# First mixing stage of a two-block kernel: decay and keys early, the triangular inverse in pieces, attention and linear-attention units in one loop

## The reference

```
p = h @ ab_w_in                              # q, k, v of the attention | r, k, v, w, a, g of the other
# differential attention, per head, causal, in blocks of 128 queries
s = q_c . k_c (c = 0, 1);  p_c = softmax(mask(s_c))
attn = p_0 - lam_full * p_1;  o = rmsnorm(attn @ v) * (1 - lam_init)
# the other one (RWKV-7 time mix): token shift with mu, then per step
decay = exp(-exp(-0.5) * sigmoid(w0 + tanh(p_w) @ w2)); a = sigmoid(a0 + p_a @ a2)
kk = normalise(k * k_k); k = k * (1 + (a - 1) * k_a)
S = S * decay - (S kk) (kk * a)^T + v k^T;   y = S r
out = (groupnorm(y) + sum(r * k * r_k) * v) * g
```

## Time and profile before

| | us |
|---|---|
| median of 3 runs | 2768.85 (2764.5 to 2778.71) |
| profiled execution, its own time | 2759.99 |
| its span in the profile | 2758.2 |
| TensorE busy in the span | 2653.2 (96%) |
| VectorE, ScalarE, GpSimd busy | 1453.7, 985.1, 528.3 |
| mean granted clock of TensorE | 0.977 |

### The profile page before, as it was taken

One profiled execution on the slowest core, in us unless ns is written; L12 is line 12 of the kernel. 1 busy time (PEld: TensorE's weight loads), 2 busy tenths in 40 slices (PEclk: granted clock), 3 DMA queues, 4 the chain that ended last, 5 costly groups with the idle time before them and its releaser, 6 DMA issues.

```text
span 2758.2 us, 32180 instructions
## 1 busy us (share of the span) xinstructions
PE 2653.2 (96%) x13236; PEld 2112.1 (77%) x13236; DVE 1453.7 (53%) x1905; ACT 985.1 (36%) x1660; POOL 528.3 (19%) x554
## 2 busy tenths in 40 slices
PE   8989998999999998899999999999999998999998
PEld 7777877788888665686788888888878745888886
DVE  8875995643434688546433334343354466533432
ACT  3235545422323533543322223222233445322221
POOL 5711001322200020101222102221002124222200
PEclk9999999999999998899999999999999989999999
DMA  4433112222232231002232332323323300222332
GB/s 154 100 96 113 62 46 69 84 100 93 96 102 93 71 99 32 28 2 69 100 100 92 95 104 92 99 98 93 102 78 122 116 16 1 78 98 99 97 93 86
DMA packets 76932, 232.19 MB, mean 84 GB/s; under 512 B 14961, under 2 KB 16241, under 8 KB 76529
## 3 DMA queue, kind: packets, MB, share of 16 engines
q1 hardware_dynamic: 64176, 212.46, 23.8%
q0 software_dynamic: 4400, 9.71, 1.6%
q10 hardware_dynamic: 8208, 7.96, 0.9%
HBM read 220.13 MB, written 5.77 MB: 82 GB/s over the span
## 4 chain that ended last, share of the span: by engine, by line
PE 78%; DVE 10%; ACT 5%; POOL 4%; issue 1%; DMA 0%; ACTq 0%; DVEq 0%; POOLq 0%
PE ps L358 78%; POOL mem L375 3%; DVE mem L375 3%; DVE part L445 2%; ACT part L433 1%; DVE mem L388 1%; PE ps L369 1%; ACT mem L509 0%; POOL mem L3269 0%; DVE mem L393 0%; DVE mem L3032 0%; DVE mem L408 0%; DVE mem L553 0%; DVE mem L634 0%; DVE mem L2167 0%
## 5 line engine op out<-in xcount | busy, mean ns | idle before, releaser
L358 PE MATMUL ps<-part,part 128*128 128x512 f32 (+1 forms) x9870 | 2249.8, 389 | 33.0 <-DVE part L445 8.5
L358 PEld LDWEIGHTS ps<-part,part 128*128 128x128 f32 x9870 | 1838.7, 189 | 439.6 <-issue 15.8
L445 DVE TENSOR_TENSOR part<-mem,part 128x1024 fp32r<-128x1024 f32 (+2 forms) x419 | 563.2, 1351 | 597.6 <-ACT part L433 597.3
L433 ACT ACTIVATE part<-mem 128x1024 fp32r<-128x1024 f32 (+2 forms) x419 | 415.6, 1003 | 241.9 <-DMA mem<-in_ffa_down 55.9
L375 DVE TENSOR_TENSOR mem<-ps,mem 128x512 f32<-128x512 f32 (+1 forms) x266 | 176.7, 664 | 297.1 <-PE ps L358 288.1
L358 PE MATMUL ps<-mem 128*64 128x64 f32 (+13 forms) x2568 | 264.5, 310 | 35.8 <-ACT mem L2385 10.3
L358 PEld LDWEIGHTS ps<-mem 128*64 128x64 f32 (+5 forms) x2568 | 180.7, 165 | 109.5 <-issue 41.5
L517 POOL TENSOR_TENSOR mem<-mem 128x512 f32<-128x512 f32 x62 | 80.6, 1300 | 713.2 <-ACT mem L509 712.2
L1669 POOL TENSOR_TENSOR mem<-mem 128x512 f32<-128x512 f32 x88 | 113.8, 1293 | 381.5 <-ACT mem L1657 381.5
L1671 POOL TENSOR_TENSOR part<-mem,part 128x512 fp32r<-128x512 f32 x88 | 113.8, 1293 | 353.0 <-ACT part L1660 353.0
L1660 ACT ACTIVATE part<-mem 128x512 fp32r<-128x512 f32 x88 | 55.6, 632 | 327.9 <-DVE mem L375 327.9
(11 more groups left out here) (191 smaller groups left out, 1182.8 us busy)
## 6 DMA issues: line engine op xcount, KB each, us to landing
mem<-in_ffa_gate SPq DMA_DIRECT2D x44, 512.0 KB, 3.3
mem<-in_ffa_up SPq DMA_DIRECT2D x44, 512.0 KB, 3.3
mem<-in_ffb_gate SPq DMA_DIRECT2D x44, 512.0 KB, 3.2
mem<-in_ffb_up SPq DMA_DIRECT2D x44, 512.0 KB, 3.3
mem<-in_ffa_down SPq DMA_DIRECT2D x32, 512.0 KB, 3.5
mem<-in_ffb_down SPq DMA_DIRECT2D x32, 512.0 KB, 3.5
mem<-in_w_odd SPq DMA_DIRECT2D x24, 512.0 KB, 3.3
mem<-in_w_ab SPq DMA_DIRECT2D x22, 512.0 KB, 3.2
```

What stands on the lines that cost most here:

```text
L358: return e.matmul(out, l, r, start=start, stop=stop, skip_group_check=True)
L433: w.e.activation(K.wts[c % NH].h[:, 0:n], K.raws[c % NR][:, 0:n], ACT.Copy).then_inc(*K_A.up(("w", c)))
L445: w.e.tensor_tensor(t.l, K.raws[c % NR][:, 0:n], t.hf, SUB).then_inc(*K.V.up(("w", c)))
```

## The change

The first stage of the second block is reordered. (1) `MIXED` puts the low-rank inputs first and the gate's last; the decay and rate products of all four groups follow chunks 2 and 3, the squares of the keys chunk 6, the spreads chunks 8 and 9, L chunks 11 to 13 and the first q chunk, the bonus the q chunks 1 to 3 and the first k chunk. Each group has its own buffers for the decay (`sets`), so that no group waits for another's. (2) The inverse's diagonal steps lie between the ropes of q and k, parts 1 to 6 ahead of the attention, parts 7 and 8 in its first step. (3) Attention and units run in one loop of 22 steps, the units four steps behind; the scores have one pair of banks, 1 and 2, which they share with `ml`; G shares bank 4 with R. The attention's probabilities lie in weight slots. The four norm products of the attention come in step 19, the spreads in step 21 and in the state loop. (4) The low parts of the eight q and k chunks are made by GpSimd.

```diff
     rows("w_ab", [8 + j for j in MIXED])
-    rows("w_ab", range(8))
+    rows("w_ab", range(8), gpsimd=True)
...
+OUT_A = 26
+DELAY = 4
+STEPS_AB = 16 + DELAY + 2
...
-        sets = [self.vt[:, i, :] for i in range(4)] + [spare[:, 0:T], spare[:, T:2 * T]]
-        self.sets = [sets[0:3], sets[3:6]]
+        q, k, vt = ([x[:, i, :] for i in range(4)] for x in (self.q, self.k, self.vt))
+        self.sets = [[q[2], q[3], spare[:, 0:T]], [vt[0], vt[1], spare[:, T:2 * T]], [vt[2], vt[3], k[0]],
+                     [k[2], k[3], k[1]]]
...
-        self.tm = raw[:, 0:1024]
+        self.tm = shuffled
...
+        self.sqa, self.ya = self.q, self.k
+        ring = [K.slots[(K.first[4] + OUT_A + 1 + i) % NH] for i in range(3)]
+        self.pr = [ring[i // 4][:, T * (i % 4):T * (i % 4) + T] for i in range(6)]
+        self.pt = [ring[1][:, 1024 + T * i:1024 + T * i + T] for i in range(2)]
+        self.dg = [K.nb[3][:, P * i:P * i + P] for i in range(3)]
...
+def ab_units_tensor(K, w):
+
     w.wait_ge(*K.V["k", "rope", 3])
...
+    for j in range(STEPS_AB):
+        u = j - DELAY
+        if j < 16:
+            ab_score_tensor(K, w, j)
+        if 0 <= u - 1 < 16:
+            rwkv_c_tensor(K, w, u - 1)
+        if 0 <= u - 2 < 16:
+            rwkv_e_tensor(K, w, u - 2)
+        if 0 <= j - 2 < 16:
+            ab_turned_probs_tensor(K, w, j - 2)
+        if 0 <= u < 16:
+            rwkv_b_tensor(K, w, u)
+        if 0 <= u - 1 < 16:
+            rwkv_d_tensor(K, w, u - 1)
+        if 0 <= j - 3 < 16:
+            ab_values_tensor(K, w, j - 3)
+        if j == 19:
+            K.take(w, ("ms", "subln"), K.V, bank=6)
+            for hd in range(4):
+                ab_subln_tensor(K, w, hd)
+        if j > 20:
+            for hd in (2 * j - 42, 2 * j - 41):
+                w.wait_ge(*K.A["rstd", ("ms", "subln")])
+                ab_rows_tensor(K, w, hd)
...
         if n == 0:
             norm_tensor(K, w, 4, K.ss)
             norm_columns_tensor(K, w, 4)
-        if n == 5:
+        if n == 2 or n == 3:
+            ab_low_tensor(K, w, 2 * n - 4)
+            ab_low_tensor(K, w, 2 * n - 3)
+        if n == 6:
             ab_heads_tensor(K, w, "kk", E.be, lambda a: K.A["kk2", a])
-        if n == 6:
-            ab_low_tensor(K, w, 0)
-            ab_low_tensor(K, w, 1)
-        if n in (8, 9, 12, 13):
-            ab_spread_tensor(K, w, "kk", (8, 9, 12, 13).index(n), E.factors)
-        if n == 10 or n == 11:
-            ab_bonus_tensor(K, w, n - 10)
-        if n == 12:
-            ab_low_tensor(K, w, 2)
-        if n == 13:
-            ab_low_tensor(K, w, 3)
+        if n == 8 or n == 9:
+            ab_spread_tensor(K, w, "kk", 2 * n - 16, E.factors)
+            ab_spread_tensor(K, w, "kk", 2 * n - 15, E.factors)
+        if n > 10:
+            ab_lower_tensor(K, w, n - 11)
     for first, name in ((0, "q"), (4, "k")):
         for o, _ in enumerate(linear(K, w, name, 4, 8, K.h, h_ready, K.A)):
             n = first + o
-            if n < 2:
-                ab_lower_tensor(K, w, n)
-            if n == 1 or n == 2:
-                ab_bonus_tensor(K, w, n + 1)
-            if n == 4 or n == 6:
-                ab_lower_tensor(K, w, n // 2)
+            if n == 0:
+                ab_lower_tensor(K, w, 3)
+            if 0 < n < 5:
+                ab_bonus_tensor(K, w, n - 1)
     K.ring(4, 5, 6, 7)
     linear_tok(K, w, "av", T, K.h, h_ready, K.A)
-    ab_attention_tensor(K, w)
...
+    ab_units_tensor(K, w)
...
+        if c == 4 or c == 5:
+            ab_rows_tensor(K, w, c - 2)
...
-    accG = K.take(w, ("G", i), K.V, bank=4)
+    accR = K.take(w, ("R", i), K.A, bank=4)
+    accG = accR[:, 256:512]
     accN = K.take(w, ("N", i), K.A, bank=5)
-    accR = K.take(w, ("R", i), K.A, bank=6)
...
-    done.then_inc(*K.P.up(("G", i)))
...
 def ab_kk_vector(K, w, a):
 
     E = K.ab
+    sg, s2, s3 = E.sets[a]
     w.wait_ge(*K.P["kk", a])
     tt(w, E.al(a), E.al(a), v4(K.acc("kk", a)), MUL, ("kk", a))
-    w.wait_ge(*K.A["rates", a])
-    tt(w, E.ka(a), E.ka(a), E.be(a), MUL)
-    stt(w, E.be(a), E.rk(a), K.pc("rk", a), E.ka(a), MUL, MUL, ("rk", a))
-
-
...
     tt(w, E.be(a), E.al(a), v4(E.aa[:, a, :]), MUL)
     w.wait_ge(*K.A["decays", a])
     tt(w, E.al(a), E.al(a), v4(s3), MUL)
     tt(w, E.be(a), E.be(a), v4(sg), MUL, ("prepared", a))
+
+
+def ab_bonus_vector(K, w, a):
+    E = K.ab
+    stt(w, v4(E.sets[a][2]), E.rk(a), K.pc("rk", a), E.ka(a), MUL, MUL, ("rk", a))
...
+def ab_units_vector(K, w):
+
+    E = K.ab
+    for j in range(STEPS_AB):
+        u = j - DELAY
+        if j < 16:
+            ab_max_vector(K, w, j)
+        if 0 <= j - 1 < 16:
+            ab_mix_vector(K, w, j - 1)
+        if j == 0:
+            ab_inverse_vector(K, w, 7)
+            ab_inverse_vector(K, w, 8)
+        if 0 <= u - 2 < 16:
+            rwkv_e_vector(K, w, u - 2)
+        if j == 20:
+            w.wait_ge(*K.P["ms", "subln"])
+            ts(w, E.rs[0:4, :], K.acc("ms", "subln")[0:4, :], 1.0 / 128, 1e-6, MUL, ADD, ("ms", "subln"))
+            recip(w, E.rs[0:4, 0:256], E.rs[0:4, 0:256])
+            recip(w, E.rs[0:4, 256:T], E.rs[0:4, 256:T], ("inverse", ("ms", "subln")))
+        if 0 <= u < 16:
+            rwkv_ml_vector(K, w, u)
+        if 0 <= u + 1 < 16:
+            rwkv_b_vector(K, w, u + 1)
+        if j == 19:
+            weights_lo(K, w, K.first[4] + OUT_A + 3)
...
-MIXED = [4, 5, 6, 7, 12, 13, 0, 8, 1, 9, 2, 10, 3, 11]
+MIXED = [12, 4, 5, 6, 7, 0, 8, 1, 9, 2, 10, 3, 11, 13]
...
-        if n == 6:
+        if n == 4 or n == 5:
+            ab_sums_vector(K, w, 2 * n - 8)
+            ab_sums_vector(K, w, 2 * n - 7)
+        if n == 7:
             rstd_vector(K, w, ("ms", "kk"), E.factors[0:8, :], K.acc("ms", "kk")[0:8, :], 1.0, 1e-12)
-        if n == 7:
             w.wait_ge(*K.A["lam"])
             tt(w, lam[:, 4:5], lam[:, 3:4], lam[:, 2:3], SUB)
             ts(w, lam[:, 5:6], lam[:, 4:5], -LAM0, None, ADD, None)
-        if n == 8 or n == 9:
-            ab_sums_vector(K, w, n - 8)
-        if n == 9 or n == 10:
+        if n == 8:
+            for a in range(4):
+                ab_keys_vector(K, w, a)
+        if 9 <= n < 13:
             ab_kk_vector(K, w, n - 9)
-        if n == 11 or n == 12:
-            ab_decayed_vector(K, w, n - 11)
-        if n == 13:
-            ab_kk_vector(K, w, 2)
+        if n > 11:
+            ab_lower_vector(K, w, n - 12)
     ab_project_vector(K, w, 14)
     stt(w, E.cos, K.cc("cos"), 0.125, K.rstd, MUL, MUL)
     stt(w, E.sin, K.cc("sin"), 0.125, K.rstd, MUL, MUL)
+    diagonal = ((14, 9), (8, 6), (5, 5), (4, 3), (2, 2), (1, 1))
     for o in range(8):
         weights_lo(K, w, c + 14 + o + 3)
         if o:
             ab_rope_vector(K, w, o - 1)
         if o == 0:
-            ab_sums_vector(K, w, 2)
-            ab_kk_vector(K, w, 3)
+            ab_lower_vector(K, w, 2)
+            ab_bonus_vector(K, w, 0)
+            ab_bonus_vector(K, w, 1)
         if o == 1:
-            ab_sums_vector(K, w, 3)
-            ab_lower_vector(K, w, 0)
-        if o == 2:
-            ab_lower_vector(K, w, 1)
-            ab_decayed_vector(K, w, 2)
-        if o == 3:
-            ab_decayed_vector(K, w, 3)
-        if o == 5 or o == 6:
-            ab_lower_vector(K, w, o - 3)
+            ab_lower_vector(K, w, 3)
+            ab_bonus_vector(K, w, 2)
+            ab_bonus_vector(K, w, 3)
         if o == 4:
             tt(w, E.cos, K.cc("cos"), K.rstd, MUL)
             tt(w, E.sin, K.cc("sin"), K.rstd, MUL)
             w.wait_ge(*K.V.now)
+        if 2 <= o < 6:
+            ab_bonus_out_vector(K, w, o - 2)
+        if o == 2 or o == 6:
+            ab_decayed_vector(K, w, 3 * (o // 4))
+        if o > 2:
+            ab_diagonal_vector(K, w, *diagonal[o - 3])
     weights_lo(K, w, c + 25)
     ab_rope_vector(K, w, 7)
     weights_lo(K, w, c + 26)
-    for part in range(2):
+    ab_diagonal_vector(K, w, *diagonal[5])
+    ab_diagonal_vector(K, w, 0, 0)
+    for part in range(1, 7):
         ab_inverse_vector(K, w, part)
-    ab_attention_vector(K, w)
...
+        if part < 3:
+            ab_decayed_vector(K, w, part)
+    weights_lo(K, w, c + OUT_A + 1)
+    ab_units_vector(K, w)
...
+        if n in (2, 3, 7, 8):
+            ab_spread_vector(K, w, (2, 3, 7, 8).index(n))
+        if n in (9, 11, 13, 15):
+            ab_y2a_vector(K, w, (n - 9) // 2)
...
+def ab_units_scalar(K, w):
+
+    E, c = K.ab, K.first[4]
+    for j in range(STEPS_AB):
+        u = j - DELAY
+        if 0 <= u - 1 < 16:
+            z = E.units[(u - 1) % 3]
+            w.wait_ge(*K.P["rh", u - 1])
+            w.e.activation(z.rh, K.acc("rh", u - 1)[:, 0:128], ACT.Copy).then_inc(*K.A.up(("rh", u - 1)))
+        if j < 16:
+            ab_exp_scalar(K, w, j)
+        if 0 <= j - 1 < 16:
+            ab_diag_scalar(K, w, j - 1)
+        if j >= 7 and j % 4 == 3:
+            ab_ob_scalar(K, w, j // 4 - 1)
+        if 0 <= u - 2 < 16:
+            ab_unit_out_scalar(K, w, u - 2)
```

(90 more changed lines are left out.)

361 lines of the change are left out of this document (157 added, 204 removed).

## The result

The changed kernel takes 2793.44 us (median of five, 2787.25 to 2798.44) against 2768.85: ratio 1.0083, interval 1.0064 to 1.0102, so 18 to 28 us slower. Predicted: 2783, range 2756 to 2806, and slower as the likeliest of the three.

What follows compares the result with a forecast made beforehand. TensorE, holding 78% of the chain that ended last, was taken as the bound. +27 us to the first maximum and -13 after it gave +14: about 2774 from the profiled 2759.99, 2783 as a median; range 2756 to 2806.

Steps and rivals of the forecast that it cites:

- (a) to (e): TensorE waits, us: 4.7 (tanh, chunk 2), 4.45 (banks, 3), 7.4 (keys' square, 6), 1.0 (root, 8), 6.5 (L banks, 12).
- (e): After chunk 12 TensorE waits 6.5 us for VectorE to empty banks 6 and 7; after chunk 13, 3.6 us.
- part 1: New order of the projections: waits and lower clock make chunk 13 end 26 us later (bounds 14 and 32).
- (c): After chunk 6 the fourth heads product needs the keys' square from ScalarE's step 6; TensorE waits 7.4 us.
- the clock: Up to chunk 13, lower granted clock after four waits, 1.4 to 2.9 us each: +7.
- Part 2: Chunk 13 to the first softmax maximum: 86.7 us plus 3 for collisions, against 88.50 now: +1.
- The +3 for collisions: Between chunk 13 and first maximum, GpSimd's low parts stretch VectorE operations: +3 us (bounds 0 and 10).
- Part 3: Merged loop of attention and units: 145.8 us against 161.45, -15.6; with state loop +2.6, net -13 (bounds -30, +8).
- Rivals (2) and (3): Merged loop: full step near 5.1 us, 2752, chance 0.13; shared banks chain, 9 us per step, 2805, chance 0.17.
- State loop: After the merged loop: two spreads (2.1) and VectorE's later steps (0.5) add +2.6 us.
- Rival (1): Waits in the projections shrink, as one ahead shortens the next: start +14, net 0, 2769, chance 0.25.

Runs made afterwards that it cites:

- E1: Changed kernel with the low parts of the eight query and key weights back on VectorE; ratio 1.0062 to the kernel before.
- E3: Changed kernel with low-rank products a chunk later, Sigmoids and sums a step later, decay exponentials behind the keys; ratio 1.0067 to the kernel before.
- E6: E5 with one low-rank product pair behind each of chunks 3 to 6, heads product behind 7, spreads behind 9 and 10; 2753.2 us against 2771.8, ratio 0.9925.
- E2: Changed kernel with VectorE's emptying of the L banks ahead of the keys' products in steps 12 and 13; ratio 1.0050 to the kernel before.
- E5: Changed kernel with E1, E2 and E3 together, L banks emptied one VectorE step earlier still, bonus operands earlier; ratio 0.9980 to the kernel before.
- E11: E6 with three of four norm products one step earlier, units five steps behind, first two spreads behind the loop; ratio 0.9951 to the kernel before.
- E8: E6 with the units three steps behind instead of four, first two spreads behind the loop; ratio 0.9952 to the kernel before.
- E7: Kernel before with only the low parts of the eight query and key weights moved to GpSimd; ratio 1.0012 to the kernel before.
- E9: E6 with the low parts of the query and key weights on GpSimd again; ratio 0.9966 to the kernel before.

## Why the prediction was right, and where its sizes were off

The forecast (a little slower, +14 in the stage) held in sign and mechanism; the measured time lies 10 us above it, inside its range.

- **(a) to (e).** Predicted 4.7, 4.45, 7.4, 1.0, 6.5 and 3.6; measured 4.80, 3.76, 7.08, 0.88, 8.47 and 3.46. Program order and durations of rows were enough. The 2 us in excess at (e) are GpSimd's low part beside the keys' products, which part 1 named and did not add (E1: 6.38). The terms listed at (c) give some 8 us behind chunk 6 and not the 10.5 that the wait was worked out from; measured are 9.8, and what the list lacks is that ScalarE's copy of chunk 5 starts 2.9 us behind that chunk (940.57 against 937.6). E3 and E6 show the causes of (a) to (c), E2 and E5 that of (e).
- **The rest of the +31.8 up to chunk 13** is the term that was mis-sized: the waits give 25.0 - 4.7 = 20.3, the clock and what else lies there 11.5, not 7. TensorE's busy time says the same (98.97 against 87.49), at a mean granted clock of 0.89 against 0.98. In all +31.8 for +26, at the edge of the bounds (14 to 32).
- **Part 2.** 91.35 us for 90. The +3 for collisions is what E1 gives in this stretch (2.9), but for a reason I had wrong: I set the bound by half of GpSimd's 20 us, while VectorE's rows grew by 14.9 us in place of 7.3 us (six of 1.22) of its own low parts. That leaves 7.6 more to do, and the path shows 2.9. TensorE waits 10.20 us ahead of the second scores, as VectorE does pieces 1 to 6 first.
- **Part 3.** -21.7 for -15.6. By its own parts: from the first maximum to unit 0 at 1123.4, 17.8 (17); twelve full steps 87.6 (90; of the 4 us added for the t = 3 steps 1.8 came true, much of it one wait of 0.84 on ScalarE in every four steps); steps 16 to 18 18.4 (19.6); the end 15.9 (19.2, where the root was covered but for 1.00 us). Rivals (2) and (3) are out: a full step is 7.4 us, not 5.1 and not 9.
- **State loop.** +6.2 for +2.6. The two spread products lie in it as said; the rest goes with the clock:

```profile
1203.27:1208.00 4.73, 4.73 (x91) 4.73 (x90) 2.50 (x5) 1.25 (x2) 0.00 (x0) 0.50 0.00 0
1208.00:1214.00 6.00, 6.00 (x94) 4.40 (x94) 1.12 (x3) 0.01 (x1) 0.00 (x0) 0.78 0.01 3
1214.00:1220.00 6.00, 6.00 (x120) 6.00 (x116) 3.88 (x7) 1.26 (x2) 0.00 (x0) 0.50 0.01 3
1220.00:1228.00 8.00, 6.43 (x183) 5.76 (x182) 5.00 (x10) 0.00 (x0) 0.00 (x0) 1.00 0.01 2
```

These are E6's windows of the state loop; a granted clock of 0.50 is the 1.2 GHz level. A state step (32 matmuls) takes 1.66 and 1.60 us in the first and third stretch and 1.21 in the kernel before, whose state loop ran at 1.00:

```profile
1222.25:1240.57 18.32, 16.36 (x465) 14.70 (x465) 6.61 (x16) 0.37 (x1) 0.00 (x0) 1.00 0.01 3
```

What lets the clock fall there is open. It fell in all profiles with the merged loop (means of 0.68 to 0.92 over the state loop), in E11 (0.85) even without a wait ahead of the spreads, and least in E8, which has the longest wait there (4.84 us). All of these have spread products ahead of and inside the state loop, the kernel before and E7 (both 1.00) have none; no run separates the two.
- **Rival (1)**, waits that shrink because one shortens the next, took place only when edits removed waits (E3: 3.0 of 8.3 us came back at (e)); in the changed kernel all stood at full length.

- **The sum.** The stage is +19.2 for +14. That it is this close is partly luck: the forecast was 5.8 us too low up to chunk 13, 1.9 up to the first maximum and 3.6 in the state loop, and 6.1 us too high in the merged loop. The stage's 5 us are half of the 10 us by which the medians lie above the forecast; the rest isn't accounted for (the stage's start alone scatters by 11 us between profiles).

So the merged loop is worth 15 us net of the state loop's growth, and the new order of the projections lost 35 us, nearly all by where single calls stand. E6 shows that the loop's gain is there to be kept.

## What to carry to other kernels

When work is moved to an earlier place in hand-ordered programs, count for each consumer what the producing engine still has in front of it in that step; with rows for the durations this gave six waits within 2 us, and shifting calls by one step removed most of them (25.0 us up to chunk 13 became 3.3 in E6). Two products that want four banks of a ring at once waited 3.76 us in both places tried; one per chunk did not wait. Work handed to an idle engine had a price on the engine beside it, and more of that price showed once the other waits were gone.

## What the runs showed of the hardware

- A GpSimd subtraction over 128x1024 (2.35 to 2.72 us in the changed kernel) beside VectorE's two-input work in SBUF cost VectorE 2.4 us on the average, as much as it took, twice what it spared (1.22). VectorE's operations that read PSUM kept their duration (692 and 691 ns in E1's table). The stretched row ends 0.1 to 0.6 us behind GpSimd's. The Trainium skill, "SBUF — State Buffer", section "Who interferes with whom", calls the shared port pair an exclusive lock; in that the trace agrees.
- What I had not expected: a VectorE row that began 1.3 us ahead of GpSimd's (1044.02 and 1045.40, again 1048.40 and 1049.74), while GpSimd's DMA issues ran, was stretched as well, to 4.3 us. A row that began behind GpSimd's was stretched too (1017.74 for 1016.81, 1.97 us for 0.75). So the prediction's reading, that whoever comes second blocks, isn't what the start times in these rows show: it is VectorE's row that grew in both orders, while GpSimd's took 2.35 to 2.41 us (2.69 and 2.72 in chunks 11 and 12). Issues alone do no harm: in E1 VectorE's rows beside them keep 0.69.
- The same loop of 1384 matmuls took 138.6 to 143.6 us at delays of four, with mean granted clocks of 0.95 to 0.90. In the two longest (E3 143.6, E9 142.6) two unit intervals of 9.1 to 9.2 us for 7.6 are most of the difference.
